# Norm statistics by a constant matrix: eleven norms of a two-block transformer kernel rewritten

## The reference

```python
def rms_norm(x, g):
    y = x32 * rsqrt(mean(x32 * x32, axis=-1) + 1e-6)
    return y * g

def modulate(h, shift, scale):
    return h * (1 + scale) + shift

# first block, 6 times:  stage(modulate(rms_norm(x, g), shift, scale))

def layer_norm(x, g, b):
    xc = x - mean(x)
    return xc * rsqrt(mean(xc * xc) + 1e-5) * g + b

# second block, 5 times: h = layer_norm(x); h = layer_norm(alpha * h + stage(h)); ...
```

## Time and profile before

| what | value |
|---|---|
| median of 3 runs | 3732.96 us (3728.23 to 3733.44) |
| the profiled execution, own time | 3734.95 us |
| its span, first to last instruction | 3733.2 us |
| mean granted TensorE clock | 0.966 of full speed |
| busy: TensorE, VectorE, ScalarE, GpSimd | 94%, 51%, 34%, 10% of the span |
| bytes read from HBM | 344.10 MB, 93 GB/s over the span |

### The profile page before, as it was taken

The page is one execution under the profiler, slowest core; times in us unless marked ns, Lnnn a source line. Parts: engine busy times, 40 slices in busy tenths (PEclk is TensorE's granted clock), DMA queues, the critical chain, the costliest instruction groups (busy, mean ns, idle before and its releaser), DMA issues.

```text
span 3733.2 us, 40477 instructions
## 1 busy us (share of the span) xinstructions
PE 3505.1 (94%) x17064; PEld 2896.1 (78%) x17064; DVE 1916.7 (51%) x2662; ACT 1265.7 (34%) x1779; POOL 373.7 (10%) x216
## 2 busy tenths in 40 slices
PE   2999999899979999999999999989999998999998
PEld 2888888788767888788777888766788876678887
DVE  8433343566656453635344333486564538656464
ACT  4322122444433222322234222334342432344242
POOL 3311001111110000000001000420100033010001
PEclk9999999899989999999999999989999999999999
DMA  5423241011115353535212232210232222012221
GB/s 193 141 80 123 85 152 63 29 35 35 34 63 174 124 198 113 190 122 176 89 66 96 92 101 96 82 53 6 68 106 97 96 74 75 6 52 98 99 96 57
DMA packets 95798, 348.83 MB, mean 93 GB/s; under 512 B 10624, under 2 KB 11136, under 8 KB 95104
## 3 DMA queue, kind: packets, MB, share of 16 engines
q1 hardware_dynamic: 94320, 343.06, 27.6%
q10 hardware_dynamic: 1296, 3.18, 0.2%
HBM read 344.10 MB, written 2.10 MB: 93 GB/s over the span
## 4 chain that ended last, share of the span: by engine, by line
PE 84%; DVE 9%; ACT 4%; POOL 1%; issue 1%; DMA 0%; SPq 0%; ACTq 0%; DVEq 0%; POOLq 0%
PE PS L341 83%; DVE CAC L1872 2%; ACT G L1111 1%; DVE ST L1679 1%; PE PS L413 1%; DVE WL L1448 1%; POOL SM L2160 1%; DVE SCR L1479 1%; ACT HH L994 1%; ACT G L982 1%; DVE PTL L1662 1%; DVE X L1843 0%; ACT PTH L1092 0%; DVE ST L1963 0%; DVE SCR L1471 0%
## 5 line engine op out<-in xcount | busy, mean ns | idle before, releaser
L341 PE MATMUL PS<-HH,WH 128*128 128x512 f32 (+1 forms) x3120 | 1194.4, 383 | 46.8 <-DVE HL L1560 21.1
L341 PE MATMUL PS<-HL,WH 128*128 128x512 f32 (+1 forms) x3120 | 1177.9, 378 | 0.0
L341 PE MATMUL PS<-HH,WL 128*128 128x512 f32 (+1 forms) x3120 | 1174.6, 376 | 0.0
L1448 DVE TENSOR_TENSOR WL<-RAW,WH 128x1024 fp32r<-128x1024 f32 x462 | 580.9, 1261 | 895.3 <-ACT WH L943 895.2
L943 ACT ACTIVATE WH<-RAW 128x1024 fp32r<-128x1024 f32 x496 | 523.2, 1057 | 1217.2 <-PE PS L341 1206.9
L341 PEld LDWEIGHTS PS<-HH,WH 128*128 128x128 f32 x3120 | 595.4, 191 | 164.0 <-DVE HL L1560 23.3
L341 PEld LDWEIGHTS PS<-HL,WH 128*128 128x128 f32 x3120 | 595.3, 191 | 109.4 <-issue 5.5
L341 PEld LDWEIGHTS PS<-HH,WL 128*128 128x128 f32 x3120 | 594.0, 190 | 108.7
L341 PE MATMUL PS<-AH,WH 128*128 128x512 f32 x1392 | 525.9, 378 | 1.7 <-DVE WL L1448 1.7
L341 PE MATMUL PS<-AL,WH 128*128 128x512 f32 x1392 | 525.5, 377 | 0.0
L341 PE MATMUL PS<-AH,WL 128*128 128x512 f32 x1392 | 523.8, 376 | 0.0
(11 more groups left out here) (277 smaller groups left out, 3288.2 us busy)
## 6 DMA issues: line engine op xcount, KB each, us to landing
RAW<-wst SPq DMA_DIRECT2D x640, 512.0 KB, 3.3
X<-xT SPq DMA_DIRECT2D x1, 2048.0 KB, 12.2
out<-X SPq DMA_DIRECT2D x8, 256.0 KB, 2.0
PTF<-cb SPq DMA_DIRECT2D x1, 1024.0 KB, 4.8
Y<-yT SPq DMA_DIRECT2D x1, 1024.0 KB, 6.9
PTF<-cb ACTq DMA_DIRECT2D x1, 1024.0 KB, 4.8
HM<-sg ACTq DMA_DIRECT2D x4, 256.0 KB, 3.7
ROPE<-rope SPq DMA_DIRECT2D x1, 512.0 KB, 4.5
```

The source lines that it names most:

```text
L341: return e.matmul(o, l, r, start=start, stop=stop)
L1448: e.tensor_tensor(lo, raw_block(s), f32(hi), ALU.subtract).then_inc(*did("dve_done", ("wlo", b)))
```

## The change

The statistics get a form in which each step is made on whole 128x512 tiles. A constant 128x128 matrix with 1/1024 everywhere, times a tile of squares, gives the mean over the partitions already spread over all of them; such products add up in one PSUM bank. ScalarE adds epsilon and takes the root, VectorE takes the reciprocal. The modulation's scale goes into the multiplication of X(k) (a scalar_tensor_tensor, STT), its shift into both halves: ScalarE writes the high half in one pass with the shift as bias, and VectorE writes (value + shift) - high half. Part of the products goes into the running stream of the last output tile (`between`). Norms in the first block after attention add only three squares on GpSimd; the other four go to TensorE. In the layer norms the approximate mean is made during tile 6, and X(6) and X(7) are centred before their last output is added; the remaining mean is subtracted by GpSimd for X(1) to X(7) (to X(5) in the last norm). The gain goes into the multiplication, the bias into the halves, and X itself gets its bias after h is done. `prepare` runs a function on one column ahead of time, so that its table is loaded. The last weight blocks of a stage are split during and after the norm's tiles.

```diff
+        def means(name, src, N, step, start, stop, *more, into=None):
+            if start:
+                _, prior = take(name, N) if into is None else hold(name, N, into)
+                for p in prior:
+                    q.wait_ge(*p)
+            q.wait_ge(*step)
+            for c in range(0, N, 512):
+                d = min(c + 512, N)
+                m = mm(bank[name][:, c:d], mean, src[:, c:d], start, stop)
...
+        def squares(st):
+            up = BEFORE[st]
+            q.wait_ge("consts")
+            means(("ms", st), ACC, tokens(st), ("acc", up, 3 if up == "at" else 6), True, False, ("acc read", st),
+                  into=0 if up == "at" else 6)
         def norm(st):
-            stat(st, [(ACC, 128, ones, ("acc", up, 6)), (G(("sq", up, 7)), 128, ones, ("sq", up, 7))], nt, 1,
-                 ("gdone", ("sq", up, 7)))
-            spread(st, nt, None, ("rs", st))
+            up, N = BEFORE[st], tokens(st)
+            for m in range(4, 8) if up == "at" else (7,):
+                means(("ms", st), G(("sq", up, m)), N, ("sq", up, m), False, m == 7, ("gdone", ("sq", up, m)))
...
+                        if st == "f11":
+                            between = center("m0", m, (5, 7, 10))
+                        elif m == 7:
+                            between = {(nf - 2, 0): lambda: squares(AFTER[st])}
...
+            def first():
+                means(("mean", st), ACC, NX, ("sum", st), True, True)
+            def second():
+                means(("v", st), A2t, NX, ("csq", st, 3), True, False, ("a2 read", st), into=7)
+            def third():
+                means(("d", st), X(6), NX, ("x", up, 6), True, False, into=6)
+                means(("v", st), ACC, NX, ("csq", st, 6), False, False, ("acc read", st))
+            return {6: {(at[0], 0): first}, 7: {(at[1], 0): second, (at[2], 0): third}}.get(m, {})
         def layer_norm(st):
+            means(("d", st), X(7), NX, ("x", BEFORE[st], 7), False, True)
+            means(("v", st), G(("ce", st, 7)), NX, ("csq", st, 7), False, True, ("gdone", ("ce", st, 7)))
...
+                lin([tile(m)], ox, None, center(f"c{l}", m, (4, 5, 7)))
# ScalarE
+            e.activation(ACC[:, 0:N], bank["ms", st][:, 0:N], ACT.Sqrt, bias=EP[:, 0:1])
...
-                a = e.activation(s[:, 0:512], s[:, 0:512], ACT.Identity, scale=mcol(l, 3 * i + 1, k, 0), bias=mcol(l, 3 * i, k, 0))
-                e.activation(hview(k, N)[0], s[:, 0:N], ACT.Copy).then_inc(*did("act_done", ("hhi", st, k)))
+                a = e.activation(hi[:, 0:512], s[:, 0:512], ACT.Identity, bias=mcol(l, 3 * i, k, 0))
+                if k >= 2:
+                    part(upto[LAST[st]], 1)
+            if st in FFNS:
+                prepare(ACT.Silu, "silu", st)
...
+                    if last and m == 7:
+                        stream(upto["mid", ("d", st, p, m)])
+                        prepare(ACT.Sqrt, "sqrt", AFTER[st])
# VectorE, RMS norm
-            stat(st, 2, N // 128, 1.0 / 1024, 1e-6)
+            e.reciprocal(ACC[:, 0:N], ACC[:, 0:N]).then_inc(*did("dve_done", ("rs", st)))
...
+                        e.scalar_tensor_tensor(out=G(use)[:, c:d], in0=src(k), scalar=mcol(l, 3 * i + 1, k, s), in1=ACC[:, c:d], op0=ALU.mult,
+                                               op1=ALU.mult)
...
+                        e.scalar_tensor_tensor(out=lo[:, c:d], in0=G(use)[:, c:d], scalar=mcol(l, 3 * i, k - 1, s), in1=f32(hi)[:, c:d], op0=ALU.add,
+                                               op1=ALU.subtract)
# layer norm: ScalarE, VectorE, GpSimd
+            e.activation(A2t[:, :], bank["d", st][:, :], ACT.Square).then_inc(*did("act_done", ("dsq", st)))
+            e.activation(ACC[:, 0:512], bank["d", st][:, :], ACT.Copy).then_inc(*did("act_done", ("dcopy", st)))
+            e.activation(A2t[:, :], A2t[:, :], ACT.Sqrt, bias=EP[:, 1:2]).then_inc(*did("act_done", ("std", st)))
...
+            e.tensor_tensor(A2t[:, :], bank["v", st][:, :], A2t[:, :], ALU.subtract)
+            shift(0)
+            e.reciprocal(A2t[:, :], A2t[:, :])
+                    e.scalar_tensor_tensor(out=X(k), in0=X(k), scalar=v2(g, k), in1=A2t[:, :], op0=ALU.mult, op1=ALU.mult)
...
+            q.wait_ge("dcopy", st)
+            for k in range(1, 8 if st != "end" else 6):
+                q.wait_ge(*(("cx", st, k) if k < 7 else ("x", BEFORE[st], 7)))
+                e.tensor_tensor(X(k), X(k), ACC[:, 0:512], ALU.subtract).then_inc(*did("pool_done", ("xs", st, k)))
```

More of the change, by code:

```diff
@@ L52 @@
 KS = (2, 3, 4, 5, 6, 0, 1, 7)
+AFTER = {before: stage for stage, before in BEFORE.items()}
 def wide(stage):
@@ L1023, in ffn @@
                             total("m0", m)
-                    stream(upto["d", st, p, m])
+                    if not last or m < 7:
+                        stream(upto["d", st, p, m])
         def attention():
@@ L1800, in fourier, with shifted, center, center_more @@
                     stream(upto["fw", m])
[L1802 to L1809 removed]
+        def shifted(st, k, done, *more):
+            c = -1024.0 / 768 / (ALPHA if st[0] == "c" else 1.0)
+            e.scalar_tensor_tensor(out=X(k), in0=bank["mean", st], scalar=c if k >= 6 else -1024.0 / 768, in1=X(k), op0=ALU.mult,
+                                   op1=ALU.add).then_inc(*did("dve_done", (done, st, k), *more))
+        def center(st, ready):
+            q.wait_ge("tile", ("mean", st))
+            q.wait_ge(*ready)
+            shifted(st, 6, "x-")
+            for k in range(4):
+                q.wait_ge("x", BEFORE[st], k)
+                shifted(st, k, "cx")
+        def center_more(st, ready):
+            for k in (4, 5):
+                q.wait_ge("x", BEFORE[st], k)
+                shifted(st, k, "cx")
+            q.wait_ge(*ready)
+            shifted(st, 7, "x-", ("free", ("mean", st)))
             q.wait_ge("cs", st, 5)
@@ L1849, in layer_norm @@
+            q.wait_ge("tile", ("v", st))
+            q.wait_ge("dsq", st)
+            e.tensor_tensor(A2t[:, :], bank["v", st][:, :], A2t[:, :], ALU.subtract).then_inc(*did("dve_done", ("var", st), ("free", ("v", st))))
+            shift(0)
+            q.wait_ge("std", st)
+            e.reciprocal(A2t[:, :], A2t[:, :]).then_inc(*did("dve_done", ("rs", st), ("free", ("d", st))))
+            q.wait_ge("rs", st)
+            q.wait_ge("vec2")
+            for k in range(9):
                 if k < 8:
-                    q.wait_ge("tile", ("sp", b))
+                    if st == "end" and k >= 6:
+                        shift(k)
@@ L2160, in rsqrt @@
             e.tensor_tensor(sm(name, b, n), sm(name, a, n), MH[:, 0:n], ALU.pow).then_inc(*did("pool_done", ("rs", name)))
-        def norm(st):
-            rsqrt(st, 0, 6 if wide(BEFORE[st]) else 4, 4 if not wide(BEFORE[st]) else 6, ("ms", st))
         def by_cos(key, s):
```

322 lines of the change are left out of this document (161 added, 161 removed).

## The result

The changed kernel takes 3747.25 us (median of 5 runs, 3745.2 to 3750.32) against 3732.96 for the kernel before (5 runs, 3728.23 to 3736.76). The ratio is 1.0041, with a 95% interval of 1.0026 to 1.0056: slower by 14.3 us where 28 us of gain were forecast, and outside the range, which ended at 3744. The interval leaves out 1, so the loss is small but clear. The profiled execution has a span of 3748.5 us against 3733.2.

What follows compares the result with a forecast made beforehand. TensorE was taken as the bound, with gains only in its unfed gaps at eleven norms. RMS norms 18.5 us plus layer norms 10.2 made 28.7 off, giving 3705; range 3692 to 3716, to 3744 with rival (a)'s upper part.

Steps and rivals of the forecast that it cites:

- That slope gives 0.15 + 511 x 0.002 = 1.2 us for 512 columns: VectorE's reciprocal in every norm, extrapolated from 153 ns at one column and 155 at two; 1.7 us for 768 columns.
- 7.2: Forecast path in us of a 512-column RMS norm, from the stage's last product to the next stage's first.
- 10.4: Forecast path in us of a layer norm: 8.1 unloaded, lengthened by three STTs running beside GpSimd's subtractions.
- The forecast's price of 11.5 us for each microsecond of reciprocal: All norms together: each microsecond the reciprocal takes was said to cost the kernel 11.5 us.
- rival (b): Reciprocal in the norms takes three to five passes, 2.5 to 3.3 us: total 3720 to 3729; chance 0.14.
- rival (a): Reciprocal in every norm takes eight passes, 4.9 us (7.2 for 768 columns): total 3738 to 3747; chance 0.20.
- The break-even that the forecast gave, 3.7 us: Reciprocal length at which the whole gain is gone; slower by 0.2% begins at 4.3 us.
- mean 3.6, shifts to 5.1, first two squares 6.5, three GpSimd adds of 1.5 give 11.0: another 1.3 of waiting: Two norms after the mixer: fourth tile's sum of squares, asked for 9.7 us after tile 5, makes TensorE wait 1.3 us.
- Rival (d): Wide products in TensorE's stream and waits at K = 8 give back the gain; doubled, 3718 us; chance 0.06.
- 2.3 us of contention: Layer norms: three STTs beside GpSimd's subtractions lose 0.65 to 0.9 us each, raising the path from 8.1 to 10.4.
- the forecast's estimate by it, 11.5 - 1.2 = 10.3: Layer-norm path if four VectorE operations each wait for a GpSimd one: 11.5 us, including 1.2 of reciprocal.
- The table loads stayed hidden: Loads for root and Silu or Sigmoid cost nothing, covered by ScalarE's idle time and TensorE's queued products; uncovered, 1.3 us each.

Runs made afterwards that it cites:

- run 1: The changed kernel with each of the eleven reciprocals replaced by a tensor_scalar of the same shape that writes a constant: 3724.01 us, ratio 0.9970.
- run 3: The changed kernel with weight-block splits queued behind residual and centring on VectorE and ScalarE in the two mixers' last product: 3729.01 us, ratio 0.9988.
- run 2: The changed kernel with root and reciprocal replaced by one ScalarE function, Abs_reciprocal_sqrt: 3707.79 us, ratio 0.9932.
- run 7: The changed kernel with one ScalarE root-and-reciprocal, centring ahead of the split, and unread TensorE products added in the norms' gaps: 3682.96 us, ratio 0.9859.
- runs 6 to 9: Changed kernel with one ScalarE root-and-reciprocal, centring ahead of the split, plus inner layer-norm subtraction on VectorE, unread TensorE products, or both: 3685.13, 3682.96, 3683.32, 3683.09 us.
- run 6: Changed kernel with one ScalarE root-and-reciprocal, centring ahead of the split, and the four inner layer norms' mean subtracted on VectorE from PSUM: 3685.13 us, ratio 0.9866.
- run 10: The changed kernel with unread TensorE products added after the statistics of its six RMS norms, nothing else: 3752.88 us, ratio 1.0055.

## Why the prediction was wrong

The forecast was 28.7 us of gain; the profiled span shows 15.3 of loss, 44 apart. Two steps of the forecast carry most of it, and two smaller terms follow.

**The reciprocal, about 19 of the 44.** The step that failed is "That slope gives 0.15 + 511 x 0.002 = 1.2 us for 512 columns". At one and two columns, 153 and 155 ns, the fixed part of the instruction dominates, and a difference of 2 ns between rows whose own times spread by more than 10 ns was multiplied by 511. The measured slope is (4948 - 3340) / 256 = 6.3 ns a column. In the six RMS norms all of the excess is on the path, as run 1 shows: 7.2 + 2.15 = 9.35 for the fourth norm, measured 9.45 (a handover in rows 4 is 0.09 and not 0.07, which is the rest). Four times 2.15 and twice 3.25 make 15.1 us. In the four inner layer norms 10.4 + 2.15 = 12.55 also meets the measured 12.58 to 12.85, but that is partly luck. Run 1 had a stand-in of 1.48 us there, near the forecast's 1.2, and its gap was 11.55, not 10.4. So the reciprocal's own share is about 1.05 us a norm, 4.2 in all, and at the last norm nothing. The forecast's price of 11.5 us for each microsecond of reciprocal was too high for the same reason.

The size, 3.35, lies just above rival (b), 2.5 to 3.3, and below rival (a), 4.9. In the prediction's own formula it is five and a half passes, 0.15 + 5.4 x 0.59; by that formula the three to five passes of (b) are 1.9 to 3.1 us and not 2.5 to 3.3. The Trainium skill ("VectorE: DVE Perf Modes", "First, the fixed hardware budget") gives a repeat count of 8 and no time; read as eight passes, as (a) did, it overstates this row. The break-even that the forecast gave, 3.7 us, was not reached: by this step alone the kernel would have stayed faster.

**The two stages after a mixer, 16 of the 44.** The step that failed: "mean 3.6, shifts to 5.1, first two squares 6.5, three GpSimd adds of 1.5 give 11.0: another 1.3 of waiting". It took the shifts to follow the mean at once. It forgot what stands ahead of them on VectorE and ScalarE: the split of a weight block whose buffer TensorE releases only at the end of tile 6. The extra length was 21.1 us, 5.2 of it forecast; run 3, which changes only that order, took 19.2 away again, 13.5 as waits and the rest as slow products behind them. Rival (d), "waits at K = 8 give back the gain", named the place, but priced it at double 1.3.

**The subtractions on GpSimd, about 5 of the 44.** This is the rest of the layer norms' gaps. The forecast put 2.3 us of contention on each, and in the changed kernel the rows show 2.0 (4.23 us for the first three STTs against 2.2 alone). That agreement is luck too, because the long reciprocal gave GpSimd time to get through part of its seven: with the reciprocal gone, run 2 shows 10.15 to 10.41 us, where the forecast's pricing gives 10.4 - 1.2 = 9.2. The Trainium skill ("SBUF — State Buffer", "Terms") calls the port pair an exclusive lock; the forecast's estimate by it, 11.5 - 1.2 = 10.3, is the better of the two there. The rows agree with it in kind: in the changed kernel such an STT took 0.74 us with GpSimd idle and mostly 1.75 beside a subtraction, with nothing between 0.81 and 1.75.

**The pace after the gap, 1.5 of the 44.** The forecast had no term for it. The sixtieth product comes later than in the kernel before behind norms 3, 4 and 5, by 0.79, 0.97 and 0.42 us, and 0.68 earlier behind norm 6. With 0.86 for the wide product in the stream, that makes the 1.67, 1.86 and 1.26 us by which the stages before norms 4 to 6 grew. Behind norm 4 the granted clock was 0.67 before and 0.50 after. It is tempting to lay this on the spreading products, 2.08 us of work ahead of the restart, which the change took out. That is not shown: behind norm 6, where they were taken out just as well, it is the other way round (windows view, the kernel before, then the changed one):

```profile
1996.15:2001.15 5.00, 5.00 (x12) 3.98 (x13) 4.69 (x8) 4.91 (x8) 0.00 (x0) 0.50 0.00 0
```

```profile
1996.11:2001.11 5.00, 5.00 (x13) 3.99 (x14) 5.00 (x8) 2.94 (x4) 0.00 (x0) 0.56 0.08 18
```

What run 7 shows is that products up to the restart keep the clock at 1.00 behind it.

These are 41 to 42 of the 44. The rest is small terms in both directions whose cause stays open: the stage before norm 2 grew by 3.3 us where 1.3 was forecast, and norm 3 came out 1.4 better than the forecast with the true reciprocal in it.

Right were: the frame (TensorE's gaps are the time; the sum of gap and stage closes to the span) and the path of an RMS norm with its handovers. The table loads stayed hidden, as forecast: the 21 prepared ones took 26.9 us, and no wait of VectorE ends on one.

## What to carry to other kernels

Before a small statistic is made wide, ask for each operation what it costs per column, and don't take that from one-column rows: here they showed the fixed part only. Until a wide row exists the upper bound has to carry a chance. When a step is moved into another engine's queue, list what stands ahead of it there and who releases that, above all where the stages are short. When an overrun meets a total exactly, ask whether a second term hid behind it: the reciprocal and GpSimd's subtractions overlapped, and their costs do not add. And the idea itself was sound: with one ScalarE instruction for root and reciprocal and the centring ahead of the split (run 5) it is 1.2% faster than the kernel before, and 1.3 to 1.4% with the further edits of runs 6 to 9, 3683 to 3691 us.

## What the runs showed of the hardware

- RECIPROCAL on VectorE costs about 6.3 ns a column: 153 ns for 128x1, 3.35 us for 128x512, 4.95 for 128x768. Beside GpSimd's subtractions it took the same (3.34 us in all five layer norms).
- On ScalarE, Abs_reciprocal_sqrt of 128x512 took 687 ns, the same as Sqrt.
- In the changed kernel's layer norms an STT with both operands in SBUF took 0.73 to 0.75 us with GpSimd idle, 0.81 or 1.75 beside GpSimd's subtractions of 128x512, and 2.9 beside its splits of 128x1024. A TENSOR_SCALAR with one SBUF operand took 0.43 and 1.48 us (run 1). With one operand in PSUM, a subtraction on VectorE took 0.69 us beside GpSimd (run 2) and 0.68 without (run 6).
- Products that nobody needs can be worth something: 2.74 us of them, where TensorE was idle for 3.2, kept the granted clock at 1.00 and brought the next sixty products in 2.0 us earlier (run 7, norm 4). Where it was idle for 6.6 us and they ended 4 us before the restart, they brought nothing (run 10).
- A wait of 5.77 us in front of the last 15 records of TensorE in a stage brought the granted clock behind it to 0.62, and they took 7.44 us instead of 4.63 (changed kernel against run 3).
